# Softmax rows of latent attention scaled by DVE ahead of the next tile's maximum, with POOL left the sums and their inverses

## The reference, cut to what matters

```python
s = (jnp.einsum('bqhd,bkhd->bhqk', qn_b, k_nope)
     + jnp.einsum('bqhr,bkr->bhqk', qr_b, k_rope)) * ATTN_SCALE
p = jax.nn.softmax(s.astype(jnp.float32), axis=-1).astype(v.dtype)
return jnp.einsum('bhqk,bkhd->bqhd', p, v)
```

## Time and profile before

| what | value |
|---|---|
| median of 3 runs | 1678.98 us (1676.52 to 1681.0) |
| the profiled execution: its time | 1674.56 us |
| its span | 1672.8 us |
| PE busy in the span | 1477.5 us (88%) |
| DVE busy | 764.5 us (46%) |
| ACT busy | 709.3 us (42%) |
| POOL busy | 507.5 us (30%) |

### The profile page before, as it was taken

The page is one execution under the profiler, slowest core; times in us unless marked ns, Lnnn a source line. Parts: engine busy times, 40 slices in busy tenths (PEclk is TensorE's granted clock), DMA queues, the critical chain, the costliest instruction groups (busy, mean ns, idle before and its releaser), DMA issues. The chain is left out here.

```text
span 1672.8 us, 20712 instructions
## 1 busy us (share of the span) xinstructions
PE 1477.5 (88%) x7744; PEld 1284.0 (77%) x7744; DVE 764.5 (46%) x1088; ACT 709.3 (42%) x1360; POOL 507.5 (30%) x457
## 2 busy tenths in 40 slices
PE   5877888778878788889899999999999999999994
PEld 1555655657777777778799999889999888999994
DVE  5412212256666666644144444555444555444443
ACT  5434343346666666533143333433333443333331
POOL 3443443148888887734300000020000002000003
PEclk8788789689999999999999999999999999999997
DMA  7432232100000000050153333334333333433320
GB/s 280 147 126 70 71 105 76 42 0 5 5 5 5 1 1 1 1 214 1 48 193 128 127 129 125 118 122 166 127 126 126 115 112 128 161 125 125 125 75 38
DMA packets 44459, 154.54 MB, mean 92 GB/s; under 512 B 5129, under 2 KB 6665, under 8 KB 44393
## 3 DMA queue, kind: packets, MB, share of 16 engines
q1 hardware_dynamic: 43096, 148.96, 25.3%
q0 software_dynamic: 1296, 4.72, 0.7%
HBM read 148.70 MB, written 4.80 MB: 92 GB/s over the span
## 5 line engine op out<-in xcount | busy, mean ns | idle before, releaser
L1630 PE MATMUL bank<-h2h,w1h 128*128 128x384 f32 x768 | 257.6, 335 | 0.5 <-DVE w1l L1559 0.5
L1630 PE MATMUL bank<-h2h,w1l 128*128 128x384 f32 x768 | 257.8, 336 | 0.0
L1630 PE MATMUL bank<-h2l,w1h 128*128 128x384 f32 x768 | 257.2, 335 | 0.0
L1477 POOL TENSOR_TENSOR x<-x,add 128x512 f32<-128x512 f32 x18 | 22.9, 1307 | 746.6 <-DVE add L1583 746.6
L869 POOL TENSOR_SCALAR prow<-prow,rs 128x1152 f32<-128x1152 f32 x64 | 205.2, 3206 | 6.3
L1641 PE MATMUL bank<-w2h,rTh 128*128 128x512 f32 x576 | 181.1, 395 | 8.4 <-DVE rTl L1570 8.4
L1641 PE MATMUL bank<-w2h,rTl 128*128 128x512 f32 x576 | 179.0, 392 | 0.0
L1641 PE MATMUL bank<-w2l,rTh 128*128 128x512 f32 x576 | 179.0, 392 | 0.0
L1514 ACT ACTIVATE rTh<-sq 128x384 fp32r<-128x384 f32 x94 | 49.3, 525 | 244.5 <-PE bank L1641 239.3
L1506 ACT ACTIVATE relu<-bank 128x384 f32<-128x384 f32 x94 | 46.2, 491 | 246.8 <-PE bank L1630 246.8
L1559 DVE TENSOR_TENSOR w1l<-w1raw,w1h 128x1024 fp32r<-128x1024 f32 x96 | 118.6, 1236 | 63.5 <-ACT w1h L1493 63.5
(11 more groups left out here) (234 smaller groups left out, 2944.5 us busy)
## 6 DMA issues: line engine op xcount, KB each, us to landing
w1raw<-in_w SPq DMA_DIRECT2D x96, 512.0 KB, 3.8
w2raw<-in_w SPq DMA_DIRECT2D x96, 512.0 KB, 4.7
ada_raw<-in_w_ada SPq DMA_DIRECT2D x48, 512.0 KB, 4.3
xin<-in_x SPq DMA_DIRECT2D x9, 512.0 KB, 3.7
x<-in_x SPq DMA_DIRECT2D x3, 1536.0 KB, 13.2
out_y<-x POOLq DMA_DIRECT2D x9, 512.0 KB, 5.1
wraw<-in_w_in SPq DMA_DIRECT2D x8, 480.0 KB, 3.5
xn<-in_w_o SPq DMA_DIRECT2D x4, 512.0 KB, 3.9
```

The lines of the kernel that those rows point to most:

```text
L1477: nc.gpsimd.tensor_tensor(k.x[:, t, cut], k.x[:, t, cut], add[:, i, :], ALU.add).then_inc(out_added, 1)
L1630: op = nc.tensor.matmul(bank[6 + s][:, 0:BN], w[0][s][x][:, c * P:(c + 1) * P], k.h2[b % 2][y_][:, c, :], start=n == 0, stop=n == 3 * DC - 1)
```

## The change

In `normalise(u)` POOL no longer scales the row. It makes the sum and its inverse, and now waits (from tile 4 on) until the row of tile u-4, which used the same slot of `rs`, has been scaled. A new function in DVE's stream, `scale_row(u)`, waits for the inverse and scales the row in place; it raises `p_ready` as L869 did. DVE calls it for tile u-1 in step u, behind the first two `low` and the context maximum and in front of `maximum(u)`; for the last tile in step 64. PE's and ACT's streams are unchanged, and so are the number and size of all transfers.

```diff
@@ POOL
                 def normalise(u):
                     s = u % 4
                     pool.wait_ge(p_exp, 2 * u + 2)
+                    if u >= 4:
+                        pool.wait_ge(p_ready, u - 3)
                     nc.gpsimd.tensor_tensor(rs[:, s:s + 1], psum[:, s, 0:1], psum[:, s, 1:2], ALU.add).then_inc(p_rs, 1)
                     pool.wait_ge(p_rs, 2 * u + 1)
                     nc.gpsimd.tensor_tensor(rs[:, s:s + 1], rs[:, s:s + 1], k.minus[:, :], ALU.pow).then_inc(p_rs, 1)
-                    pool.wait_ge(p_rs, 2 * u + 2)
-                    nc.gpsimd.tensor_scalar(prow[:, s, :], prow[:, s, :], rs[:, s:s + 1], None, ALU.mult).then_inc(p_ready, 1)
@@ DVE
+                def scale_row(u):
+                    s = u % 4
+                    dve.wait_ge(p_rs, 2 * u + 2)
+                    nc.vector.tensor_scalar(prow[:, s, :], prow[:, s, :], rs[:, s:s + 1], None, ALU.mult).then_inc(p_ready, 1)
+
@@ DVE's loop
                     if ctx_now(u - 1, "scores"):
                         maximum_ctx(h)
+                    if 1 <= u <= NU:
+                        scale_row(u - 1)
                     if u < NU:
                         maximum(u)
```

## The result

The changed kernel takes 1697.37 us (median of 4 runs, 1694.67 to 1698.29); the kernel before, measured with it, 1679.01 us (4 runs, 1676.52 to 1681.0). The ratio is 1.0107, with a 95% interval of 1.009 to 1.0125: **slower by 18.4 us**, where 9.9 had been forecast. The direction was right and the time lies in the stated range of 1677 to 1704, but the size was nearly double.

What follows compares the result with a forecast made beforehand. No engine was full, so waits set the pace, with DVE's loop and PE's wait for POOL's row deciding. Terms -7.7 - 0.6 + 7.0 + 5.2 + 1.7 + 4.3 = +9.9 us gave a median of 1688.9 us, range 1677 to 1704.

Steps and rivals of the forecast that it cites:

- the forecast's own band: Whole kernel: 1684 to 1693 us, by the uncertainty of the windows and the scaling's price; chance 0.57.
- POOL and DVE in each other's way: Rival, attention loop: POOL's L859 starts first and 21 scalings cost 0.73 us more each, +15.3, 1704 us; chance 0.08.
- DVE's loop: Attention: exponential, high parts, low parts, maximum, next exponential set the pace, with PE's scores beside it.
- the windows in front of the maxima: DVE's idle before each maximum plus 0.08 us overlap; a scaling delays the maximum by 0.74 us less that window.
- the walk: Step-by-step sum of delays over the attention's tiles: +7.0, +5.2, +1.7 and +4.3 us added, -7.7 and -0.6 removed.
- the tail's -0.6: Tail: the last pair's transposes no longer wait 0.57 us for POOL's row, -0.6 us.
- The removed wait: Second tile of heads 1 to 6: PE's transposes stop waiting for POOL's row, gain 1.28 us six times, -7.7.
- The cover of the inverse: Before each scaling: POOL's inverse, some 0.9 us after the exponential, is ready before the low parts end, 1.6 to 1.8 after.
- 6.1, 6.4 and 5.7 in the steps 26, 28 and 30, unchanged: Even steps inside a head: wide windows hide the scaling, so maximum-to-maximum times in us stay the same.
- PE did not catch up the delays: Rival, inside heads and at first tiles: the next wide window absorbs later maxima, 1671 to 1675 us, faster; chance 0.11.
- the single rate: Rival, scaling on DVE: each takes 1.28 us instead of 0.74, about +40, 1719 us; chance 0.03.

Runs made afterwards that it cites:

- no_scaling: The change with the row scaling left out on every engine, transposes waiting for the inverse alone, output not normalised; ratio 0.9972 to the kernel before.
- mixed_side_later: Kernel before, with PE's next-head piece issued behind the following scores and DVE scaling only the row of a head's last tile; ratio 0.9841, 1649.25 us.
- behind_side: The change, with even tiles' rows scaled at the end of DVE's odd step, behind the side work; ratio 0.999 to the kernel before.
- after_key_first: The change, with DVE's low part of the keys (L1009) moved directly behind the maximum; ratio 0.9993 to the kernel before.
- before_late_key: Kernel before, POOL still scaling, with one spare DVE instruction in front of the keys' low part (L1009) in two steps of eight; ratio 1.0181.
- before_key_first: Kernel before, POOL still scaling, with DVE's low part of the keys (L1009) directly behind the maximum; ratio 0.9931.

## Why the prediction was right, and where its size was off

The direction came from the mechanism named. That the time lies in the range is in part luck: 1697.4 is above the forecast's own band of 1684 to 1693, and the range reached up to 1704 for a rival (POOL and DVE in each other's way) that did not come about.

- *DVE's loop paces the attention, and the windows in front of the maxima are what counts.* Right. The scaling takes 0.81 us (0.82 said) and 0.73 of the stream (0.74 said). 54 of the 55 steps without a fall of the clock lie within 0.05 us of the walk; its 10.5 us inside the loop (9.9 with the tail's -0.6) came out as 9.8 in both profiles. The tail was 0.5 us shorter than in the first profile of before; the third profile of before is as short without the change, so this gain is not clear of the spread.
- *The removed wait.* Right for the steps that it names: -1.28 at six second tiles, and POOL's row is in nobody's way. But -7.7 is not what the removal gives by itself: in no_scaling, which removes the same wait and adds nothing, five falls (7.8 us) ate more than half of the 13.1.
- *The cover of the inverse.* Right: of 64 scalings only the first, that of tile 0, waited for POOL (2.5 us, where DVE had waited for scores before). mixed_side_later shows what it costs when POOL is still busy.
- *"6.1, 6.4 and 5.7 in the steps 26, 28 and 30, unchanged."* This is the step that failed. A later maximum makes PE wait longer at the projection behind it, 1.84 instead of 1.24 us and 2.35 to 2.6 instead of 1.84 to 2.08, and I counted such a wait at its length alone, with the clock of 0.99 of the earlier trace rows taken as given. Behind 14 of 24 such waits PE's clock fell and the scores came 1.1 to 1.6 us late. The length of the wait explains only a part of them. At the third tile it goes with it: 5 falls in 12 at 1.84 us, none in 12 at 1.12 us in no_scaling and behind_side. At the fifth tile it does not: 9 in 12 at 2.33 to 2.63 us with the change, and 9 in 12 at the old 1.84 and 2.08 us without the delay. With the slow steps of head 0 counted too, the two profiles of the change hold 13.3 and 10.1 us of them, the three of before 1.6, 3.2 and 1.5. The difference of the means, 11.7 - 2.1 = 9.6, and the walk's 9.3 (9.8 less the tail's 0.5) make 18.9, where 18.4 was measured. (So close a match is luck: the stretch ahead of the loop, which the change does not touch, differs by up to 6.9 us among the five profiles.) The missing term was as large as the whole sum. That short waits take the falls away with all scalings still on DVE is shown by after_key_first; that falls need no scaling, by no_scaling and before_late_key.
- *The rivals.* PE did not catch up the delays. The scaling did not run at the single rate. POOL and DVE did meet, but the other way round: the scaling started first, was never longer than 0.82 us, and it was L859 that got longer, up to 1.40 us instead of 1.00. Nobody waited more for L859 than before (ACT 2.4 us, in both). DVE, then POOL:

```profile
534.18 0.81 DVE L1028 TENSOR_SCALAR prow<-prow,rs 128x1152 f32<-128x1152 f32 x1
...
534.46 1.39 POOL L859 TENSOR_TENSOR qTl<-qf,qTh 128x384 fp32r<-128x384 f32 x1 [0.84 <-ACT qTh L912]
```

**What stays open.** That PE's clock fell is shown, and what it cost; why it falls at one place and not at its like is not. Behind waits of 1.84 to 2.08 us at the fifth tile it fell 5 times in 6 in no_scaling, 4 in 6 in behind_side, and 0 in 18 in the kernel before. The missing wait for POOL's row does not settle it either: behind that same wait of 1.9 us the clock fell once in 18 in the kernel before, and 4 times in 6 in before_key_first. The heads differ in length too (44.5 to 44.7 us in the kernel before, 42.5 in no_scaling without a fall), but no run varies that alone. A version with PE kept busy in the wait was not tried. The Trainium skill (TensorE: Matmul & The Clock Gate, "Part 1: The HAM clock gate") says that the clock is 1.2 GHz after idleness and 2.4 GHz when busy, and that when it changes is not tied to the start of the program. That agrees with the same kernel falling in other heads in its second profile (among the fifth tiles 20, 28, 36, 44 and 52 at first, then 12, 28, 36 and 52).

## What to carry to other kernels

Before moving work to an engine that is "46% busy", write down the idle window in front of the one instruction that it will stand ahead of, step by step; a price set against such windows gave this loop to 0.05 us a step, wherever PE's clock held. Look also at where PE waits some 2 us: behind such a wait the clock can fall and cost 1.5 us more, and here a change that only took work away, no_scaling, brought that about. A granted clock near 1 in the profile before is no promise. Here the better cure was to reorder PE, so that its scores do not stand behind a wait for DVE (ratio 0.988 with POOL scaling as before). Giving DVE then only the one row in eight that POOL has no time for had the lowest median (0.984), but its gain over the reordering alone is not shown.

## What the runs showed of the hardware that I had not expected

The spare DVE instruction of before_late_key (64 partitions, 1024 columns, SBUF to SBUF, without a dependence) took anything from 0.69 to 1.80 us, and what POOL was doing when it started decides which:

```profile
L1071 DVE TENSOR_SCALAR spare<-ropeq x14: 690/1186/1802, 365.1 to 672.7; 64x1024 f32<-64x1024 f32 x14
```

Six times POOL ran nothing beside it: 0.69 us. Six times it started while POOL was in L860, the low part of a query piece: 1.19 to 1.30. Twice, in head 0, it started while POOL scaled a row: 1.80 and 1.64. The longest of them, then one beside L860, each with POOL's instruction:

```profile
363.14 3.22 POOL L870 TENSOR_SCALAR prow<-prow,rs 128x1152 f32<-128x1152 f32 x1
365.10 1.80 DVE L1071 TENSOR_SCALAR spare<-ropeq 64x1024 f32<-64x1024 f32 x1
...
426.60 0.99 POOL L860 TENSOR_TENSOR qTl<-qf,qTh 128x384 fp32r<-128x384 f32 x1
426.85 1.30 DVE L1071 TENSOR_SCALAR spare<-ropeq 64x1024 f32<-64x1024 f32 x1
```

POOL's row ends at 363.14 + 3.22 = 366.36, that is 1.26 us after the spare instruction started, and this takes 1.80 - 0.69 = 1.11 us more than alone. L860 ends 0.74 us after it started, and it takes 0.61 more. In all eight cases the surplus is the rest of POOL's instruction less 0.13 to 0.15 us, while the row and L860, which had started first, keep their length. The change shows the same thing turned round: the scaling of 534.18 ends 0.53 us after L859 starts, L859 takes 0.39 longer, and no scaling took more than 0.82.

So of such a pair the one that starts second is longer by about the rest of the other. A kernel that shares such rows between the two engines, as one might do to halve both loads, has to count with that; by these rows a scaling on DVE that starts just behind one on POOL would be some 3 us longer (an estimate from L870's 3.2 us; no run had such a pair). The Trainium skill (SBUF — State Buffer, "SBUF: two separate sides") describes an exclusive lock that either engine holds for a whole instruction. These rows agree with it, but for the 0.13 to 0.15 us.
